# Gated-delta stages: another order of the steps of the four compute engines

## The chip, the cores and the metric

The kernel runs on one core of one Trainium2 chip. The metric is device time in microseconds (us). Before the change it is 2894.6 us, the median of three runs (2892.34 to 2895.38).

## What is computed

Two small transformers, one after the other, on 256 tokens of width 1024, in float32. The first has four layers, each a SwiGLU feed-forward, a mixer and a second feed-forward; the mixers are gated delta, stick-breaking attention, sparse attention and again gated delta. The second has two layers of another mixer and a squared-ReLU feed-forward. The change touches the two gated-delta mixers alone. Of one:

```python
proj = h @ w_in                                             # 1024 -> q, k, v, z (1024 each), b, a (8 each)
qkv = silu(causal_depthwise_conv(proj[..., :3072], conv_w)) # 4 taps
q, k = l2norm(q) * 128 ** -0.5, l2norm(k)
beta = sigmoid(b); g = -exp(a_log) * softplus(a + dt_bias)
# chunk by chunk: decay = exp(segment sums of g) below the diagonal
lower = where(strict, beta * (k @ k.T) * decay, 0)
sol = triangular_solve(lower + eye, [v * beta, k * beta * exp(g_cum)])
# u = u_in - w @ state; o = q_dec @ state + (q @ k.T * decay) @ u; state = state * g_tot + k_dec.T @ u
o = rmsnorm(o, norm_g) * silu(z)
return o @ w_out
```

## The kernel before

**Stages.** The program is a list of 16 stages (line 3142 on); the gated-delta stages are the second and the eleventh. Each compute engine has, for each stage, a written-out list of steps; `run` (line 237) walks it and advances one generator ("lane") per word. A lane's `yield` ends a step. Engines meet only at semaphores, and each engine works its own queue strictly in the order of its list. What stands behind an instruction that waits does not start.

**The W lane.** Weights come in pieces of 1 MB through a ring of five buffers. For each piece SyncE loads `raw`, ScalarE makes `hi` (line 638), VectorE the rest `lo` (line 656; GpSimd at line 676 for five late pieces of a gated-delta stage), and TensorE multiplies in three products. On TensorE a W step is half a piece: in the q, k and v columns 24 matmuls of 256 columns (lines 503 to 505, piece by piece in `tensor_cols`), in the z and output columns 12 matmuls of 512 (lines 430 to 432). On ScalarE and VectorE every other W step prepares the piece that is three pieces ahead. A stage has 21 pieces, so 42 W steps: W1 to W10 make k and the two gate columns, W11 to W18 q (q0, q2, q4, q6, two steps each), W19 to W26 v, W27 to W34 z, W35 to W42 the output.

**PSUM banks.** TensorE takes one of eight banks for every product it starts (`take`, line 212): the next one in a ring, skipping only banks that are still being filled. A bank that is full but not yet read is not skipped. TensorE then waits until its reader is done. So which earlier product a step waits for follows from the order of TensorE's list, and it changes when the list does.

**Steps of the gated-delta lanes.** `E.1` to `E.12` (VectorE line 1596, ScalarE line 1408) read one projected pair out of its bank: VectorE multiplies by the row norm (`cin`, line 1603), which frees the bank, ScalarE does the first tap, VectorE three taps for two columns (line 1609). E.1 to E.4 are k, E.5 to E.8 are q0, q2, q4, q6, E.9 to E.12 are v. `nk` and `nq` normalise k and q: the squares on ScalarE, a column sum on TensorE (line 1328), a root on ScalarE, the product on VectorE (line 1647). `c0` to `c3` are the four chains of the triangular solve, one for four heads of one half of the tokens; their steps are: .1 decay (VectorE 1671 and 1674, ScalarE's exponentials), .2 the product k k (VectorE 1684, then ScalarE's four copies into `goz`, called Z copies here), .3 to .6 the rest of the inverse. `inv.1` on VectorE (line 1718) transposes `goz` once the Z copies of all four chains are made, and GpSimd's `inv` (line 1786) then solves the small diagonal blocks. `inv.2` closes that. `kT` turns k; `rows` turns v; `qk` is q k; `a0` and `a1` apply the result; `gates` are the scalars per token and head.

Of the kernel before, what the change touches and what calls it, by code (L numbers as in the profile page):

```python
# [1231 lines left out]


GDN_PE = """
x1 W W rbc rbc W W W W W gates W W W gates gates gates gates W W c0 W c2 nk nk nk c3 W nk c0 nk W W c1 c2 kT c1 c3 W W
W W W W W kT W W nq nq nq W nq W W nq W W qk qk rows W W rows rows rows qk W W c2 c0 c1 c0 c2 c0 c1 c0 c2 c1 a0 c3 c2
a0 c3 a0 c3 c1 a0 a1 a0 c3 a1 a1 qk a0 a0 a1 W a1 W W a1 a1 W W W W next W gates gates nk nq
"""
GDN_ACT = """
x1 W W W rbc rbc E E ba W W gates gates E W W gates W W E W W nk E W W gates gates gates W W nk nk E nk nk c0 c2 W W  # L1240
c3 c2 c0 c1 c3 c1 E W W W W E W W kT E nq E nq W W E nq kT nq E nq sv W W Z W W rows rows c0 c2 c1 c3 Z c2 c0 rows
rows c1 gate W W c3 a0 a0 a0 a0 a0 a1 a1 a1 a0 a0 W W a1 a1 W W W W a1 a1 W W W W next W gates nk nq
"""
GDN_DVE = """
x1 clear rbc W W W E E gates W W gates E gates W W gates E W W gates gates W W E c2 c0 nk nk nk nk E nk nk c0 c3 W W
c2 c1 c3 c1 W W inv W W E W W E E W W E nq nq nq W W E nq E W W nq nq qk inv qk c0 qk c2 c1 c0 c2 c0 c1 c3 c0 gates c2
a0 c1 a0 c2 c3 a0 c3 c1 a0 a1 a0 a1 c3 a0 qk a1 a0 a1 a1 a1 a1 W W W W W W W W W W W W out out next W W out W W rbc W
"""
GDN_POOL = """
clear c0 inv W W W W W W W W W W W W W W W W W W W W W W W W W W W c2 c1 c3 W W W W W W W W W W W W W W W  # L1250
"""


# [1929 lines left out]
```

## Time and profile before

| | |
|---|---|
| median of three runs | 2894.6 us |
| span of the profiled execution, first to last instruction | 2891.6 us |
| TensorE busy | 2851.9 us (99%) |
| VectorE busy | 1795.2 us (62%) |
| ScalarE busy | 1578.0 us (55%) |
| GpSimd busy | 452.6 us (16%) |
| mean granted TensorE clock | 0.997 |

The profile is of one execution. Its device time is not listed apart from its span, which is 3.0 us below the median of the runs. In the rows PE is TensorE, DVE VectorE, ACT ScalarE, POOL GpSimd. A row gives start, length, engine, source line, operation, output and input, and in square brackets how long the engine had been idle and who released it. The first gated-delta stage covers about 193 to 371 us of the span, the second 1665 to 1843 us, 1472.6 us later.

### The profile page before, as it was taken

The page shows a single profiled execution, that of the slowest core. Times are in us where ns is not written, and L with a number is a line of the kernel's source. Part 1 is how long each engine was busy: PE and PEld are TensorE (multiplying, and loading weights), DVE is VectorE, ACT ScalarE, POOL GpSimd, SP SyncE. Part 2 cuts the span into 40 slices and gives each one's busy share as a digit, 9 for nine tenths or more (in the row PEclk, how much of TensorE's full clock was granted, in tenths as well). Part 3 has the DMA queues.
Part 4 walks back from the last instruction along what each step waited for, and adds up shares of the span by engine and source line. Part 5 has one row for each costly group of instructions (what it writes and reads, how often), then busy time and mean ns, then how long its engine had stood idle before and what let it go on. Part 6 is the DMA issues. An engine that isn't in the chain of part 4 may idle for free.

```text
span 2891.6 us, 35970 instructions
## 1 busy us (share of the span) xinstructions
PE 2851.9 (99%) x14255; PEld 2419.0 (84%) x14255; DVE 1795.2 (62%) x2190; ACT 1578.0 (55%) x1982; POOL 452.6 (16%) x700
## 2 busy tenths in 40 slices
PE   9999999999999999999999999999999999999998
PEld 7888888888988888878888898888888888888887
DVE  5558666565666556466556487566675665775664
ACT  5448854544554454565444388643566463566462
POOL 1203512021002112041202107121000020000020
PEclk9999999999999999999999999999999999999999
DMA  8764267576548677537767653476645686645684
GB/s 277 234 191 129 88 218 239 195 247 214 173 155 245 214 227 238 181 117 225 227 207 241 200 159 117 133 247 212 200 147 174 214 278 220 194 146 176 217 278 158
DMA packets 397047, 574.90 MB, mean 199 GB/s; under 512 B 20016, under 2 KB 248624, under 8 KB 396880
## 3 DMA queue, kind: packets, MB, share of 16 engines
q1 hardware_dynamic: 372624, 508.62, 54.7%
q0 software_dynamic: 23680, 62.95, 7.0%
q8 instruction: 112, 1.84, 0.3%
q10 hardware_dynamic: 576, 1.05, 0.1%
q14 instruction: 55, 0.45, 0.1%
HBM read 540.03 MB, written 32.51 MB: 198 GB/s over the span
## 4 chain that ended last, share of the span: by engine, by line
PE 87%; DVE 6%; ACT 4%; issue 1%; DMA 1%; SPq 0%; POOL 0%; DVEq 0%; ACTq 0%
PE ps L430 26%; PE ps L432 26%; PE ps L431 26%; PE ps L616 2%; DVE lo L656 2%; DVE qkv L1609 2%; PE ps L503 1%; PE ps L505 1%; PE ps L504 1%; ACT goz L1400 1%; PE ps L587 1%; ACT hi L638 1%; PE ps L603 1%; ACT sl L1400 1%; ACT qkv L1400 0%
## 5 line engine op out<-in xcount | busy, mean ns | idle before, releaser
L656 DVE TENSOR_TENSOR lo<-raw,hi 128x2048 fp32r<-128x2048 f32 (+3 forms) x473 | 1052.6, 2238 | 451.0 <-ACT hi L638 451.0
L638 ACT ACTIVATE hi<-raw 128x2048 fp32r<-128x2048 f32 (+2 forms) x487 | 907.4, 1871 | 766.6 <-DMA raw<-in_ffn_w_gu 283.7
L430 PE MATMUL ps<-hi,xh 128*128 128x512 f32 (+1 forms) x2208 | 865.8, 392 | 3.3 <-DVE xl L812 2.4
L432 PE MATMUL ps<-hi,xl 128*128 128x512 f32 (+1 forms) x2208 | 858.4, 389 | 0.0
L431 PE MATMUL ps<-lo,xh 128*128 128x512 f32 (+1 forms) x2208 | 857.8, 388 | 0.0
L430 PEld LDWEIGHTS ps<-hi,xh 128*128 128x128 f32 x2208 | 415.0, 188 | 88.2 <-DVE lo L656 4.1
L432 PEld LDWEIGHTS ps<-hi,xl 128*128 128x128 f32 x2208 | 414.7, 188 | 85.8
L431 PEld LDWEIGHTS ps<-lo,xh 128*128 128x128 f32 x2208 | 415.1, 188 | 84.0 <-issue 1.0
L430 PE MATMUL ps<-hi,hhh 128*128 128x512 f32 x704 | 274.6, 390 | 0.0
L432 PE MATMUL ps<-hi,hhl 128*128 128x512 f32 x704 | 274.0, 389 | 0.0
L431 PE MATMUL ps<-lo,hhh 128*128 128x512 f32 x704 | 273.9, 389 | 0.0
L1009 POOL DMA_DIRECT2D hhr<-turned x352 | 191.3, 550 | 377.6 <-DMA turned<-hhf 368.7
L503 PE MATMUL ps<-xh,hi 128*128 128x256 f32 x672 | 195.9, 292 | 8.2 <-DVE cin L1603 8.2
L504 PE MATMUL ps<-xl,hi 128*128 128x256 f32 x672 | 191.8, 285 | 0.0
L505 PE MATMUL ps<-xh,lo 128*128 128x256 f32 x672 | 191.6, 285 | 0.0
L1005 POOL DMA_DIRECT2D turned<-hhf x88 | 49.7, 565 | 792.7 <-DVE hhf L993 792.3
L432 PEld LDWEIGHTS ps<-hi,hhl 128*128 128x128 f32 x704 | 132.1, 188 | 27.5
L431 PEld LDWEIGHTS ps<-lo,hhh 128*128 128x128 f32 x704 | 132.2, 188 | 27.2
L430 PEld LDWEIGHTS ps<-hi,hhh 128*128 128x128 f32 x704 | 132.2, 188 | 27.2
L1113 ACT ACTIVATE sg<-ps,st 128x256 f32<-128x256 f32 x176 | 78.8, 470 | 119.4 <-PE ps L432 119.2
L1028 DVE TENSOR_TENSOR hhl<-hhr,hhh 128x512 fp32r<-128x512 f32 x88 | 60.4, 687 | 128.0 <-ACT hhh L1017 99.2
L503 PEld LDWEIGHTS ps<-xh,hi 128*128 128x128 f32 x672 | 130.6, 194 | 10.5 <-DVE cin L1603 8.6
(440 smaller groups left out, 3403.3 us busy)
## 6 DMA issues: line engine op xcount, KB each, us to landing
raw<-in_ffn_w_gu SPq DMA_DIRECT2D x348, 512.0 KB, 4.8
raw<-in_ffn_w_down SPq DMA_DIRECT2D x80, 1024.0 KB, 5.0
raw<-in_w_ff SPq DMA_DIRECT2D x64, 1024.0 KB, 5.4
raw<-in_w_in SPq DMA_DIRECT2D x60, 1024.0 KB, 5.1
raw<-in_gdn_w_in SPq DMA_DIRECT2D x32, 1024.0 KB, 5.5
turned<-hhf POOLq DMA_DIRECT2D x88, 256.0 KB, 4.5
hhr<-turned POOLq DMA_DIRECT2D x352, 64.0 KB, 4.0
raw<-in_sb_w_in SPq DMA_DIRECT2D x12, 1024.0 KB, 5.1
```

The lines of the kernel that those rows point to most:

```text
L430: e.matmul(o, a1, r1, start=kk == 0, stop=False)
L431: e.matmul(o, a1, r2, start=False, stop=False)
L432: i = e.matmul(o, a2, r1, start=False, stop=kk == kts - 1)
L503: e.matmul(o, a1, x1, start=kk == 0 and q == 0, stop=False, skip_group_check=True)
L504: e.matmul(o, a1, x2, start=False, stop=False, skip_group_check=True)
L505: i3 = e.matmul(o, a2, x1, start=False, stop=kk == 7, skip_group_check=True)
L616: i = k.e.transpose(o, lhs(h), k.m.C(C_ID)) if turn else k.e.matmul(o, lhs(h), rhs(h), start=True, stop=True)
L638: k.e.activation(k.m.hi[q % RING][:, 0:n], k.m.raw[q % RING][:, 0:n], ACT.Copy).then_inc(*k.up("act_piece_hi", ("hi", q)))
L656: k.e.tensor_tensor(m.lo[i][:, 0:n], m.raw[i][:, 0:n], m.hi[i][:, 0:n].bitcast(F32), ALU.subtract).then_inc(*k.up("dve_piece_lo", ("split" ...
L1009: k.e.dma_start(f.raw[32 * b:32 * b + 32, c + 1, :].rearrange("i (a r) -> i a r", a=4), rows).then_inc(*k.up(f"dma_fetch{c % 3}", *([("fet ...
L1028: k.e.tensor_tensor(f.turned(f.low, c), f.back(c), f.turned(f.high, c).bitcast(F32), ALU.subtract).then_inc(*k.up("dve_turned_lo", ("hT", ...
L1113: k.e.activation(r["sg"][i][:, :], b.ps[:, 0:256], ACT.Silu, scale=m.st[:, 16 + t:17 + t]).then_inc(*k.up("act_ffn_silu", ("silu", g, c, t)))
```

## The change

All four lists of the gated-delta stages are replaced. Each engine has the same steps as before, in the same number, and within a lane in the same order; only the way in which the lanes are interleaved differs.

```diff
@@ -1232,22 +1232,23 @@
 
 
 GDN_PE = """
-x1 W W rbc rbc W W W W W gates W W W gates gates gates gates W W c0 W c2 nk nk nk c3 W nk c0 nk W W c1 c2 kT c1 c3 W W
-W W W W W kT W W nq nq nq W nq W W nq W W qk qk rows W W rows rows rows qk W W c2 c0 c1 c0 c2 c0 c1 c0 c2 c1 a0 c3 c2
-a0 c3 a0 c3 c1 a0 a1 a0 c3 a1 a1 qk a0 a0 a1 W a1 W W a1 a1 W W W W next W gates gates nk nq
+x1 W W rbc rbc W W W W W gates W W W W W gates gates gates gates c0 W nk nk W c2 nk c3 nk nk W c2 c0 c1 W c3 kT c1
+W kT W W W W W W nq nq W nq W nq W qk W nq W W W W qk W rows qk rows rows rows W W c0 c2 c1 c0 c2 c0 c3 c1 c0 c2 a0
+c3 c1 a0 c2 a0 c3 c1 a0 a1 a0 c3 a1 a1 qk a0 a0 a1 W a1 W W a1 a1 W W W W next W gates gates nk nq
 """
 GDN_ACT = """
-x1 W W W rbc rbc E E ba W W gates gates E W W gates W W E W W nk E W W gates gates gates W W nk nk E nk nk c0 c2 W W
-c3 c2 c0 c1 c3 c1 E W W W W E W W kT E nq E nq W W E nq kT nq E nq sv W W Z W W rows rows c0 c2 c1 c3 Z c2 c0 rows
-rows c1 gate W W c3 a0 a0 a0 a0 a0 a1 a1 a1 a0 a0 W W a1 a1 W W W W a1 a1 W W W W next W gates nk nq
+x1 W W W rbc rbc E E ba W W gates W W E gates gates W W E W W nk E W W nk W W gates gates gates nk E nk W W c0 c2
+nk c0 c3 c2 c1 c3 c1 E W W E W W kT E nq W W E kT W W nq nq W W E nq W W E nq sv Z rows rows c0 c2 c3 c1 Z c0 c2
+rows rows c1 W W c3 W W gate a0 a0 a0 a0 a0 a1 a1 a1 a0 a0 a1 a1 a1 a1 W W W W W W next W W W gates nk nq
 """
 GDN_DVE = """
-x1 clear rbc W W W E E gates W W gates E gates W W gates E W W gates gates W W E c2 c0 nk nk nk nk E nk nk c0 c3 W W
-c2 c1 c3 c1 W W inv W W E W W E E W W E nq nq nq W W E nq E W W nq nq qk inv qk c0 qk c2 c1 c0 c2 c0 c1 c3 c0 gates c2
-a0 c1 a0 c2 c3 a0 c3 c1 a0 a1 a0 a1 c3 a0 qk a1 a0 a1 a1 a1 a1 W W W W W W W W W W W W out out next W W out W W rbc W
+x1 rbc clear W W W E E gates W W gates E gates W W E gates W W gates gates W W E c0 c2 nk nk nk E nk c3 nk c0 c2 nk
+W W c1 c3 c1 W W W W inv E E E W W E W W nq nq nq nq E W W nq W W gates E nq qk qk inv c0 c2 c1 qk c0 c2 c0 c3 c1
+c0 c2 a0 c1 a0 c2 c3 a0 c1 a0 c3 a1 a0 c3 a1 a0 a1 a0 qk a1 a1 a1 a1 out W W W W W W W W W W W W out next out W W W
+W W rbc
 """
 GDN_POOL = """
-clear c0 inv W W W W W W W W W W W W W W W W W W W W W W W W W W W c2 c1 c3 W W W W W W W W W W W W W W W
+clear c0 c2 inv W W W W W W W W W W W W W W W W W W W W W W W W W W W c1 c3 W W W W W W W W W W W W W W W
 """
 
 
```

Positions by the number of W steps ahead of a step, before and after, of those that the text below speaks of. TensorE: kT.2 23 and 17; gates.5 10 and 12; nq.2 25 and 23; qk.1 30 and 26; rows.1 30 and 32. ScalarE: nk.5, c0.1 and c2.1 15 and 17; E.12 25 and 29; gate 29 and 33. VectorE: c2.2 (13 to 11), inv.1 (15 to 17), E.8 and E.9 (19 to 17), E.12 (23 to 25), out.1 (37 to 25). GpSimd: c2.1, 27 to 0 and ahead of `inv`.

## Rows read from the trace of the kernel before

**Rows 1.** Busy time, share and instructions of each engine, whole span.

```profile
PE 2851.9 (99%) x14255; PEld 2419.0 (84%) x14255; DVE 1795.2 (62%) x2190; ACT 1578.0 (55%) x1982; POOL 452.6 (16%) x700
```

**Rows 2.** Waits of TensorE, whole span: us in total, times, longest.

```profile
PE ps L503 <- DVE cin L1603: 8.2, 2, 4.1
...
PE ps L1319 <- DVE ga L1633: 1.6, 2, 0.8
...
PE ps L1328 <- ACT sy L1400: 1.0, 3, 0.6
```

**Rows 3.** Timeline of TensorE, 248 to 270 us: start, length.

```profile
250.07 0.36 PE L503 MATMUL ps<-xh,hi 128*128 128x256 f32 x1
...
261.55 0.28 PE L505 MATMUL ps<-xh,lo 128*128 128x256 f32 x1
265.95 0.58 PE L503 MATMUL ps<-xh,hi 128*128 128x256 f32 x1 [4.12 <-DVE cin L1603]
...
269.26 0.28 PE L503 MATMUL ps<-xh,hi 128*128 128x256 f32 x1
```

**Rows 4.** Timeline of VectorE, 246 to 266 us.

```profile
246.30 2.28 DVE L656 TENSOR_TENSOR lo<-raw,hi 128x2048 fp32r<-128x2048 f32 x1
...
255.82 1.13 DVE L1684 SCALAR_TENSOR_TENSOR sl<-ps,ga,sl 128x128 f32<-128x128 f32 x4 [3.04 <-ACT sl L1400]
...
261.88 1.25 DVE L1718 STREAM_TRANSPOSE gow<-goz 128x1024 f32<-128x1024 f32 x1 [2.73 <-ACT goz L1400]
263.05 2.25 DVE L656 TENSOR_TENSOR lo<-raw,hi 128x2048 fp32r<-128x2048 f32 x1
265.22 0.68 DVE L1603 TENSOR_TENSOR cin<-ps,rbc 128x512 f32<-128x512 f32 x1
```

**Rows 5.** Timeline of ScalarE, 239 to 262 us.

```profile
239.06 0.91 ACT L1400 ACTIVATE qkv<-cin,vec 128x256 f32<-128x256 f32 x2 [0.57 <-DVE cin L1603]
239.88 0.67 ACT L1400 ACTIVATE sy<-ps,const 128x512 f32<-128x512 f32 x1
...
242.35 0.62 ACT L1400 ACTIVATE sl<-sl 128x512 f32<-128x512 f32 x1
...
244.53 1.90 ACT L638 ACTIVATE hi<-raw 128x2048 fp32r<-128x2048 f32 x1
...
249.65 5.49 ACT L1400 ACTIVATE goz<-sl 32x256 f32<-32x256 f32 x8 [2.18 <-DVE sl L1684]
255.16 0.63 ACT L1400 ACTIVATE sl<-sl 128x512 f32<-128x512 f32 x1
...
256.31 5.53 ACT L1400 ACTIVATE goz<-sl 32x256 f32<-32x256 f32 x8
```

**Rows 6.** Stretches of the second stage: busy us by engine, PEclk, DMA, GB/s.

```profile
1732.00:1742.00 10.00, 5.89 (x37) 5.68 (x36) 6.94 (x10) 5.84 (x8) 5.34 (x11) 0.75 0.46 154
1742.00:1752.00 10.00, 10.00 (x79) 10.00 (x79) 8.84 (x13) 7.35 (x12) 8.75 (x17) 0.91 0.34 107
```

**Rows 7.** Timeline of TensorE, 310 to 319 us: last z piece, first chain step.

```profile
310.64 0.48 PE L430 MATMUL ps<-hi,xh 128*128 128x512 f32 x1
...
316.21 1.95 PE L616 MATMUL ps<-sl,sl 128*128 128x128 f32 x16
318.66 1.16 PE L616 MATMUL ps<-sl,sl 128*128 128x128 f32 x8 [0.51 <-ACT zs L1400]
```

**Rows 8.** Timeline of ScalarE, around 310 and 357 us.

```profile
310.63 7.27 ACT L1400 ACTIVATE sl<-gow 32x128 f32<-32x128 f32 x16 [0.33 <-DVE gow L1727]
...
357.39 1.55 ACT L897 ACTIVATE goh<-ps,vec 128x256 fp32r<-128x256 f32 x4
```

**Rows 9.** Timeline of VectorE at 306 us: the sum that closes the inverse.

```profile
306.15 4.45 DVE L1727 TENSOR_TENSOR gow<-gow 128x512 f32<-128x512 f32 x1
```

**Rows 10.** Timeline of GpSimd, 255 to 310 us.

```profile
255.22 1.29 POOL L1783 TENSOR_TENSOR sl<-sl,const 128x512 f32<-128x512 f32 x1 [10.32 <-ACT goz L1400]
...
305.44 4.60 POOL L676 TENSOR_TENSOR lo<-raw,hi 128x2048 fp32r<-128x2048 f32 x1 [1.63 <-ACT hi L638]
```

## The prediction, made before the changed kernel was run

> **What bounds the kernel now.** I read the busy shares first: TensorE is busy for 2851.9 us, 99% of the span [rows 1]. No order of steps can shorten its work; what can change is the time in which it waits, and the slower clock behind a long wait. So I read its waits next [rows 2]. The longest in a gated-delta stage, 8.2 us in two times, is of a projection matmul (line 503) for VectorE's `cin`, one in each of the two stages. The timeline shows it [rows 3]: the matmul before it starts at 261.55, the next at 265.95, where 0.12 us is the spacing of the others (96 matmuls, W17 to W20, lie between 250.07 and 261.55). Until 269.26 fifteen matmuls start 0.22 us apart: the lower clock level costs 3.31 - 15 x 0.12 = 1.5 us. In the second stage the clock is low for longer: granted 0.75 over one stretch of 10 us and 0.91 over the next [rows 6]. At the two levels of 2.4 and 1.2 GHz, 0.25 x 10 / 0.5 = 5.0 us and 0.09 x 10 / 0.5 = 1.8 us were low, some of it idle.
>
> What ended the wait, on VectorE's queue [rows 4]: W21 (v2) takes the bank that q4 (W15, W16) had filled, and q4 is read by E.7. E.7's `cin` stands behind a weight split (263.05), and that behind inv.1's transpose, which had waited 2.73 us for ScalarE's Z copies, over at 256.31 + 5.53 = 261.84 [rows 5].
>
> **The change, the decisive part: kT.2.** kT.2 moves on TensorE from behind W23 to behind W17. I counted banks through both lists. Before, it took the bank of c2's kk product, read long ago; now the ring gives it the bank after q6's (W17), and that one holds q4, which only E.7's `cin` reads. W21 now takes c0's kk bank, which is read at once, and W19 that of c2. So the same event, E.7's `cin`, releases TensorE in both orders. Before, W18, W19 and W20 were done by then. Now they are behind it.
>
> Call the release R. Before, R = 265.95. The work that is moved behind it is three W steps, 72 matmuls x 0.12 = 8.65 us (kT.2 itself is only exchanged against the place that it had). The change breaks even at this point if R comes 8.65 us earlier.
>
> When is R? E.7 follows inv.1, and inv.1 the sixteen Z copies of four chains. I follow ScalarE from E.6, whose `cin` comes at nearly the same time in both orders, to 239.06 [rows 5]. Queue in the new order until the first Z copies: E.6 0.82, root 1.24 (half of 242.35 - 239.88), weight `hi` 1.81, c0.1 and c2.1 2.18, root 1.24: 7.3, so 246.4. VectorE has c0's product at 246.2: after E.6's taps (241.8) come two normalisations of 0.6, c3's decay of 2.1 and the product, 1.13 [rows 4]; and the split of 246.30 [rows 4], which stood ahead of c2.2, is now behind both. So ScalarE's wait of 2.18 us [rows 5] is gone, and the first Z copies start at 246.4 instead of 249.65. From there ScalarE has 16 copies, 5.49 + 5.53 = 11.0, the exponentials of c3, 1.05, and of c1, 1.15 (256.31 - 255.16): to 259.6. VectorE's products of c3 and c1 are ready in time (c1's at about 254.9) and its two splits (2 x 2.2) end near 259.3. Then transpose 1.2, `cin` 0.7 with no split between, and the semaphores: R = 261.7. It gains 2.2 from the split and 2.1 from the Z copies, 4.25 in all, and I need 8.65. Net +4.4 us in each stage. The two ends for R: nothing gained by the Z copies, 263.8, net +6.5; Z copies with another 2 us less, 259.7, net +2.4. I take the middle since every term has a row.
>
> The wait itself becomes long, from 253 or so to 261.7, 8 to 9 us. The lower clock level behind it: the rows show 1.5 us lost behind a wait of 4.1 us, and more in the second stage behind the same wait [rows 3, 6], so its length is not what sizes the loss. I take the loss as before, 0 more; if it were in proportion to the wait, 1.5 to 2 more each stage.
>
> On that the Trainium skill has a rule (TensorE: Matmul & The Clock Gate, section What's actually happening): the clock falls to half after idling and returns once the engine has been busy for a while, so a longer wait costs no more slow matmuls behind it. By that the sum stays +4.4; by proportion it would be near +6. The unequal losses behind equal waits speak for the rule, and the sum does without it.
>
> **The parts costed at nothing.** Whatever is ahead of R on TensorE is worth nothing. That holds for gates.5 behind W12 (it removes a wait of 0.8 us each, [rows 2]) and for nk.5, now ahead of c0.2: its sum must wait about 2 us for ScalarE. Both end in the long wait. Without that cover they would be -0.8 and +2. GpSimd's c2.1 ahead of `inv`: GpSimd was idle 10.32 us before c0's [rows 10], so it fits. Behind `inv` it spares 1.8 us, but ScalarE's copies of the finished inverse into the chains (310.63, [rows 8]) waited for the closing sum, not for GpSimd, so 0; with that cover gone, up to -1.8.
>
> The closing sum took 4.45 us [rows 9] beside GpSimd's split of 4.60 [rows 10]. Now that split waits for E.12, whose taps end near 306, and the sum comes at 312 to 313.5. The Trainium skill (SBUF — State Buffer, section SBUF: two separate sides) says that a VectorE operation with two SBUF inputs and a GpSimd operation that reads SBUF exclude each other for a whole instruction; the trace agrees (4.45 us for a sum that ends with GpSimd's split at 310.04). By that rule the sum comes at 313.5, by free flow at 312. ScalarE gets to its copies at 314.7 either way, so neither changes the sum.
>
> **Behind R.** Being late, TensorE no longer waits for ScalarE's squares (0.6 and 0.2 us in the first stage, 1.0 in three times over both [rows 2]): -0.5 to -0.8. I take -0.7. Then each W step's split must be ready. VectorE now does E.7, E.8, E.9 in a row, and E.9 needs W20: 261.7 + kT.2 0.6 + 8.65 + slow clock 1.5 to 2 = 272.8. The splits that TensorE needs at W25, W27, W29 and W31 end by my walk at 280.7, 289.3, 299.1 and 302.4, (E.9's taps and a split; E.10 and a split; two normalisations, E.11 and a split; one more of each), and TensorE is there at 286, 293.6, 299.8 and 305.3. W29's has 0.7 us to spare. Cost 0; if VectorE is 1 to 3 us later, up to +2.5.
>
> The last z steps end at 320.0 instead of 316.21 [rows 7]. The chain's first product then finds its operand: ScalarE starts the 7.27 us of copies at 314.7, held by rows.2 (TensorE does rows.1 behind W32, at 312), ends at 322.0, does Z.2 and the copy for c0.4, 323.9. TensorE arrives at c0.4 at 323.0 and waits 0.9, where before it waited 0.5 [rows 7] and again 0.4 near this place: the same. From here on the chain steps interleave with one or more others between a product and its user as before: 0, bounds -0.5 to +0.5.
>
> At the end: VectorE's out.1 now stands ahead of one split for the next stage (2.3 us, needed only some 5 us later): 0. ScalarE's `hi` for the last output piece moves behind a1.7: `goh` 1.55 [rows 8], `hi` 1.9, GpSimd's split 4.6 [rows 10] are 8.05 us, while TensorE does three W steps of half of (316.21 - 310.64), 8.35. It just fits: +0.1, up to +1.
>
> **Sum.** Each stage +4.4 - 0.7 + 0.1 = +3.8. Both stages: +7.6. The profiled span goes from 2891.6 to 2899.2 us. The span is 3.0 us below the median of the runs; I let that difference stand: 2902.2 us.
>
> **Rivals.**
> 1. *A pile-up behind R.* VectorE and GpSimd, pushed behind W20 and E.12, miss W29, W31 or W33. Speaks for it: 0.7 us to spare, and taps that are slower beside GpSimd's `inv`. Against: ScalarE and VectorE have gaps to catch up in. +2.5 to +6 a stage more: 2907 to 2914.
> 2. *The delay is absorbed, no change within 0.2%.* R comes at 260 (-1.7 each), or the chain steps behind W34, which wait for nothing TensorE does late, come without their 0.9. 2 x (3.8 - 1.7 to 2.6) = +2.4 to +4.2: 2897 to 2899.
> 3. *Faster: R comes before its price.* Place: `cin` of E.7. It decides at R = 265.95 - (8.65 - 0.7 + 0.1) = 257.9. The Z copies would have to end at 255.8, and their own 13.2 us to start at 242.6, before the exponentials that feed them are made; R = 256.6 would give -1.3 a stage, 2892.0 in all. Only if kT.2's bank weren't q4's would it happen: then TensorE meets no gate, 4.1 + 1.5 to 2.2 + 0.7 a stage, about -13 in all: 2881. Against it: the ring gives bank after bank, and I find no step that would shift it.
>
> Chances: the forecast 0.60, rival 1 0.12, rival 2 0.21, rival 3 0.07. A measurement here tells about 0.2% (5.8 us) from no change. The forecast's own range is 2898 to 2907; its part below 2900.4 goes to "same", so slower 0.68, same 0.26, faster 0.06. The range that should hold the time 8 times in 10 is 2896.5 to 2909: it leaves out rival 3, most of rival 1, and takes in both ends for R (2 x (2.4 - 0.6) = +3.6 and 2 x (6.5 - 0.6) = +11.8).
>
> **What would show it.** In the changed kernel's trace TensorE should wait 8 to 9 us, twice, in front of a transpose of `qkv` (line 616), released by `cin` of line 1603, and no longer in front of line 503. E.7's `cin` should start at 261.0 and end at 261.7. The Z copies should start near 246.4 and end near 259.6. The last z matmul should start near 320. The waits of line 1319 should be gone, one of line 1328 of about 2 us should be there ahead of W15. The prediction is wrong if the wait is elsewhere, if R is before 259 or after 264, or if TensorE waits again for splits (line 656 or 676) between 273 and 320.

## The result, and the profile after

The changed kernel takes 2914.2 us (median of five runs, 2912.5 to 2914.4), against 2894.6 before (now also five runs): ratio 1.0070, 95% interval 1.0059 to 1.0081. It is slower, as forecast, but by 19.6 us where I forecast 7.6, and outside the range of 2896.5 to 2909. Behind the changed list the lines of the code have numbers one higher than before.

The busy times answer to [rows 1]; TensorE's work has not grown. Its waits (us in total, times, longest) answer to [rows 2].

```profile
PE 2854.1 (98%) x14255; PEld 2422.4 (83%) x14255; DVE 1793.2 (62%) x2190; ACT 1576.8 (54%) x1982; POOL 442.8 (15%) x700
```

```profile
PE ps L616 <- DVE cin L1604: 15.1, 2, 7.6
PE ps L616 <- ACT zs L1401: 11.8, 2, 6.0
...
PE ps L1329 <- ACT sy L1401: 3.7, 3, 1.2
```

The first line is the wait that I forecast. The second isn't: 6.0 us in each stage, for ScalarE's Z.2, where before it was 0.5 us [rows 7]. TensorE's timeline in the first stage has both, answering to [rows 3, 7]:

```profile
260.54 1.11 PE L616 MATMUL ps<-const,qkv 128*128 128x128 f32 x4 [7.56 <-DVE cin L1604]
...
265.72 0.33 PE L505 MATMUL ps<-xh,lo 128*128 128x256 f32 x1
265.89 0.28 PE L503 MATMUL ps<-xh,hi 128*128 128x256 f32 x1
...
282.02 1.10 PE L1329 MATMUL ps<-sy,const 128*128 128x512 f32 x2 [1.22 <-ACT sy L1401]
...
320.59 0.39 PE L432 MATMUL ps<-hi,xl 128*128 128x512 f32 x1
326.79 4.44 PE L616 MATMUL ps<-sl,sl 128*128 128x128 f32 x21 [5.81 <-ACT zs L1401]
```

Kernel before, the same two places of the chains (end of z on TensorE; VectorE's first reading of a chain product), and VectorE's first steps of inv.2:

```profile
315.99 0.39 PE L432 MATMUL ps<-hi,xl 128*128 128x512 f32 x1
```

```profile
303.96 0.87 DVE L1723 TENSOR_SCALAR goz<-gov,const 128x512 f32<-128x512 f32 x2
...
321.51 0.69 DVE L1660 SCALAR_TENSOR_TENSOR sl<-ps,sl 128x512 f32<-128x512 f32 x1 [0.98 <-PE ps L616]
```

So the last z matmul starts 320.59 - 315.99 = 4.6 us late, and the chain's product is read 332.57 - 321.51 = 11.1 us late (row below). The first matmul of the stage behind starts at 386.21 instead of 375.13, again 11.1: it is all there by the first chain product, 4.6 ahead of it and 6.5 in front of it. In the second stage the same two places stand at +2.2 and +8.8, counted from the delay that the first left: less was lost anew ahead of the chains, and 6.6 at them. Sum 19.9; the spans differ by 19.8 (2911.4 and 2891.6).

Why less ahead of the chains in the second stage? Mostly the clock. Counted at 0.12 us a matmul, the slow ones behind the wait lost 1.5 us before (15 of them) and 2.1 after (21) in the first stage, but 2.4 before (24, from 1738.56 to 1743.81) and 1.1 after (10, from 1744.99 to 1747.25) in the second. That is 1.9 of the 2.4 us between +4.6 and +2.2.

What ended the second wait is on VectorE, ScalarE and GpSimd, changed kernel, answering to [rows 9], [rows 8] and [rows 10]:

```profile
258.67 1.25 DVE L1719 STREAM_TRANSPOSE gow<-goz 128x1024 f32<-128x1024 f32 x1 [0.25 <-ACT goz L1401]
259.83 0.65 DVE L1604 TENSOR_TENSOR cin<-ps,rbc 128x512 f32<-128x512 f32 x1
...
310.16 0.69 DVE L1711 TENSOR_TENSOR qkD<-ps,qkD 128x512 f32<-128x512 f32 x1 [3.99 <-PE ps L616]
310.77 3.15 DVE L1724 TENSOR_SCALAR goz<-gov,const 128x512 f32<-128x512 f32 x2
313.95 1.25 DVE L1726 STREAM_TRANSPOSE gow<-goz 128x1024 f32<-128x1024 f32 x1
315.24 3.68 DVE L1728 TENSOR_TENSOR gow<-gow 128x512 f32<-128x512 f32 x1
...
332.57 0.69 DVE L1661 SCALAR_TENSOR_TENSOR sl<-ps,sl 128x512 f32<-128x512 f32 x1 [3.97 <-PE ps L616]
```

```profile
318.95 7.07 ACT L1401 ACTIVATE sl<-gow 32x128 f32<-32x128 f32 x16 [3.14 <-DVE gow L1728]
326.05 1.26 ACT L1401 ACTIVATE zs<-ps,st 128x512 f32<-128x512 f32 x2
```

```profile
305.05 4.99 POOL L676 TENSOR_TENSOR lo<-raw,hi 128x2048 fp32r<-128x2048 f32 x1 [11.59 <-DVE qkv L1610]
309.98 0.52 POOL L1782 MEMSET sl<- 128x512 f32 x1
...
312.19 1.45 POOL L1784 TENSOR_TENSOR sl<-sl,const 128x512 f32<-128x512 f32 x1
313.59 4.77 POOL L676 TENSOR_TENSOR lo<-raw,hi 128x2048 fp32r<-128x2048 f32 x1
```

inv.2 is the multiplications, the transpose and the closing sum. The multiplications take 3.15 us instead of 0.87, beside GpSimd's clears and chain steps. The sum takes 3.68 us and ends at 318.9, just behind GpSimd's *second* split (313.59 + 4.77 = 318.36), which had started 1.65 us ahead of it. ScalarE's copies, held by the sum, run from 318.95, and Z.2 comes behind them.

What put the two side by side is in part argued. inv.2 starts 6.8 us later than before (310.77 against 303.96), behind a `qk` product that TensorE makes only behind W31. With c2.1 gone from GpSimd's queue the second split starts some 1.7 us earlier (a clear and a chain step, 309.98 to 311.70); with c2.1 in its place it would start near 315.3 by that estimate, and the sum started at 315.24. Which of the two would have come first isn't shown: no run has GpSimd's old list beside the other new ones.

Why TensorE needs Z.2 for its first chain products (c0.3 and c2.3) is again the ring of banks. Counted through both lists: before, the products of c2 and c0 take banks of `qk` and `rows`, read early, and only c1's takes a bank of z's second half, which Z.2 reads. In the new order c0's and c2's products themselves get the two banks of that half.

The clock around both waits, by the windows (busy us by engine, PEclk, DMA, GB/s):

```profile
250.00:260.00 10.00, 2.98 (x25) 2.78 (x24) 9.37 (x19) 8.36 (x15) 2.24 (x3) 0.78 0.26 90
260.00:270.00 10.00, 9.46 (x60) 9.46 (x61) 6.18 (x13) 3.62 (x5) 8.22 (x23) 0.71 0.24 60
321.00:326.00 5.00, 0.00 (x0) 0.00 (x0) 0.00 (x0) 4.73 (x12) 0.00 (x0) 0.78 0.69 208
326.00:331.00 5.00, 4.21 (x21) 4.21 (x22) 2.48 (x4) 2.28 (x5) 0.00 (x0) 0.53 0.00 2
```

TensorE idles in the third stretch, and in the fourth it works at 1.2 GHz almost throughout.

### The profile page after: what moved, and what is told of

The parts are those of the page before. It is cut to its first block, busy times and chain, and to the rows that moved or that the text cites. A ratio compares the mean times of both kernels' runs of the same rounds, so it can differ in the third digit from the quotient of the medians.

```text
span 2911.4 us, 35976 instructions
## 1 busy us (share of the span) xinstructions
PE 2854.1 (98%) x14255; PEld 2422.4 (83%) x14255; DVE 1793.2 (62%) x2190; ACT 1576.8 (54%) x1982; POOL 442.8 (15%) x700
## 4 chain that ended last, share of the span: by engine, by line
PE 90%; ACT 4%; DVE 4%; issue 1%; DMA 1%; SPq 0%; POOL 0%; DVEq 0%; ACTq 0%
PE ps L430 26%; PE ps L432 26%; PE ps L431 26%; PE ps L616 3%; PE ps L503 2%; PE ps L504 2%; PE ps L505 2%; DVE lo L656 1%; ACT goz L1401 1%; DVE qkv L1610 1%; PE ps L587 1%; ACT hi L638 1%; ACT sl L1401 1%; PE ps L603 1%; ACT qkv L1401 0%
```

## The experiments

The theory: two gates in each stage, each a bank in the ring. One is kT.2 for E.7's `cin`. The other is the first chain products for Z.2, and Z.2 is late since inv.2 runs beside GpSimd. The rival: the delay of kT.2 alone costs everything, and the wait at the chains is only its echo. The runs come from three rounds, in which the kernel before took 2893.0, 2893.5 and 2893.2 us; between rounds the ratios are compared, not the times. The fences of the edits show only the places that change, and with the edits line numbers shift by up to six.

To move a bank without moving any work, TensorE gets a word `skip`, which passes over one bank of the ring:

```diff
+    def skip():
+        for _ in range(script.count("skip")):
+            k.c.next += 1
+            yield
```

**kt_skip: one bank passed over ahead of kT.2.**

```diff
 GDN_PE = """
 ...
-W kT W W W W W W nq nq W nq W nq W qk W nq
+W skip kT W W W W W W nq nq W nq W nq W qk W nq
```

> The changed kernel (2914.2 us) with one bank of the ring passed over ahead of kT.2 on TensorE, so that kT.2 no longer takes the bank that holds q4; all lists as changed. Theory 1, the bank gate at kT.2 carries a good part of the slowdown: the wait of 7.6 us in front of kT.2 is gone, a shorter one (4 to 5 us) comes in front of nq.2's sum, the last z matmul starts 4 to 6 us earlier, and the time falls by 7 to 11 us to 2903 to 2907. Theory 2, the late end of the inverse and of ScalarE's copies sets the time and TensorE only waits for it in one place or another: the wait in front of the chain's first products grows by what is won, and the time stays at 2911 to 2915.

Measured 2910.0 (ratio to before 1.0053, 1.0038 to 1.0067). TensorE, first stage:

```profile
275.61 2.04 PE L1328 MATMUL ps<-sy,const 128*128 128x512 f32 x2 [4.57 <-ACT sy L1405]
...
316.38 0.39 PE L432 MATMUL ps<-hi,xl 128*128 128x512 f32 x1
323.31 2.93 PE L616 MATMUL ps<-sl,sl 128*128 128x128 f32 x12 [6.54 <-ACT zs L1405]
```

The 7.6 us are gone, and z ends 4.2 us earlier. But 4.57 us come back at nq.2's sum, and at the chains TensorE waits 6.54 us instead of 5.81, so that the first chain product starts 3.5 us earlier and the next stage 2.65 (383.56 against 386.21). The second wait doesn't go with the first: it is no echo. The gain over both stages is 0.0017, some 5 us where I expected 7 to 11, and the intervals of this run and of the changed kernel overlap.

**et_skip: banks passed over ahead of the chain products alone.**

```diff
-rows rows W W c0 c2 c1 c0 c2 c0 c3
+rows rows W W skip skip c0 c2 c1 skip skip skip c0 c2 c0 c3
```

> The changed kernel with two banks passed over ahead of c0.3 and three ahead of c0.4 on TensorE, so that the first three chain products (c0, c2, c1 ET) take banks whose readers are long done, and not those of z's second half, which Z.2 reads. Theory 1, the banks of z hold these products back: the wait of 5.8 us falls to about 0.5 in front of the first and shorter ones behind it, the slow clock behind it is gone, X1 of c0 starts about 3 us earlier; 2906 to 2909. Theory 2, the operands (all sixteen copies of the inverse end at 326.05) hold the chain back anyway: under 1.5 us a stage, 2911 to 2914.

Measured 2914.9 (1.0074, 1.0057 to 1.0091): no gain. TensorE's waits and its timeline in the first stage say why:

```profile
PE ps L616 <- DVE qkD L1716: 9.9, 2, 4.9
```

```profile
319.84 1.13 PE L616 MATMUL ps<-sl,sl 128*128 128x128 f32 x8
321.61 1.13 PE L616 MATMUL ps<-sl,sl 128*128 128x128 f32 x8 [0.65 <-issue]
...
327.67 6.87 PE L616 MATMUL ps<-sl,sl 128*128 128x128 f32 x40 [4.93 <-DVE qkD L1716]
```

I had miscounted by one: c1's product now took the bank of the third `qk`, which VectorE reads behind inv.2. The edit took away one gate and made another, so it tells nothing of the gate's price. It does tell what held the first two products: with other banks they start at 319.84 and 321.61, right behind z, while ScalarE is still making the sixteen copies (317.95 to 325.04). In the changed kernel it was the bank that they waited for, not the operand.

**inv_first: inv.2 ahead of the second `qk` on VectorE.**

```diff
-nq qk qk inv c0 c2 c1 qk
+nq qk inv qk c0 c2 c1 qk
```

> The changed kernel with inv.2 ahead of the second qk step on VectorE, as before the change; nothing else. Theory 2, the inverse ends late because inv.2 stands behind a product that TensorE makes only behind W31, and then runs beside GpSimd's splits (3.15 and 3.68 us where 0.87 and 0.7 would do): the closing sum ends near 311 instead of 318.9, ScalarE starts its copies near 315.3, set by rows.2, Z.2 comes 3.6 us earlier, and TensorE's wait falls from 5.8 to 2 us; 2914.2 - 2 x (3.6 to 4.5) = 2905 to 2907. Theory 1 alone (banks, not the inverse) would leave 2912 to 2914, since Z.2 would be held by something else.

Measured 2913.3 (1.0067, 1.0052 to 1.0082), no gain clear of the scatter. In the first stage inv.2 starts 5.5 us earlier and ends 0.9 us earlier. VectorE, then GpSimd:

```profile
305.22 6.57 DVE L1723 TENSOR_SCALAR goz<-gov,const 128x512 f32<-128x512 f32 x2
...
313.11 4.91 DVE L1727 TENSOR_TENSOR gow<-gow 128x512 f32<-128x512 f32 x1
```

```profile
304.18 4.99 POOL L676 TENSOR_TENSOR lo<-raw,hi 128x2048 fp32r<-128x2048 f32 x1 [10.32 <-DVE qkv L1609]
...
312.88 4.58 POOL L676 TENSOR_TENSOR lo<-raw,hi 128x2048 fp32r<-128x2048 f32 x1
```

The same three instructions take 12.8 us. In the second stage of the same execution the closing sum begins 0.35 us ahead of the split instead of 0.23 behind it:

```profile
1795.66 0.94 DVE L1727 TENSOR_TENSOR gow<-gow 128x512 f32<-128x512 f32 x1
```

```profile
1796.01 5.06 POOL L676 TENSOR_TENSOR lo<-raw,hi 128x2048 fp32r<-128x2048 f32 x1
```

There it takes 0.94 us and not 4.91, and the wait at the chains is 2.63 us, where in the first stage it is 5.78. Moving inv.2 up the queue gains nothing by itself, as GpSimd's instructions come beside it there too; what counts is which of the two starts first. (The profiled execution, at 2910.4 us, is the fastest of the four; the others took 2912.7 to 2914.1.)

**all3: these three edits together.**

> The changed kernel with all three edits: bank passed over ahead of kT.2, banks passed over ahead of c0.3 and c0.4, inv.2 ahead of the second qk on VectorE. If the two bank waits and the late inv.2 are the whole of the slowdown, their gains add: 2888 to 2897, about the time before the change. If something else in the lists costs time (ScalarE's order of E.12 and rows), it stays at 2900 or more.

Measured 2906.8 (1.0045, 1.003 to 1.006). The gates of et_skip (4.93 us at c1's product) and of kt_skip (4.6 at nq.2) are both still there.

**u_wait: inv_first, and GpSimd's late splits wait until the closing sum is done.**

```diff
-pool_pieces(k, plan, g, ("conv", g, 22))
+pool_pieces(k, plan, g, ("U", g))
```

> The changed kernel with inv.2 ahead of the second qk on VectorE, and GpSimd's late weight splits held until the closing sum of the inverse is made (they wait for that sum instead of for E.12's taps). Theory 3: VectorE's three steps of inv.2 take 14 us because they run beside GpSimd's split, chain steps and second split, which the late E.12 has moved onto them; with GpSimd idle they take 2.8 us (0.87, 1.25, 0.7), the closing sum ends near 308, ScalarE's copies start at about 315 behind rows.2 and end at 322, TensorE's first chain product starts near 322.8 instead of 326.8 and without the slow clock behind it: 5 to 6 us a stage, 2902 to 2905. If something else makes inv.2 late, the steps stay long and the time stays at 2910 to 2914.

Measured 2906.8 (1.0047, 1.0032 to 1.0062). VectorE and GpSimd:

```profile
306.04 0.88 DVE L1723 TENSOR_SCALAR goz<-gov,const 128x512 f32<-128x512 f32 x2
...
308.23 0.69 DVE L1727 TENSOR_TENSOR gow<-gow 128x512 f32<-128x512 f32 x1
```

```profile
309.00 4.58 POOL L676 TENSOR_TENSOR lo<-raw,hi 128x2048 fp32r<-128x2048 f32 x1 [15.60 <-DVE gow L1727]
```

With GpSimd idle the three take 0.88, 1.25 and 0.69. ScalarE's copies now start at 315.6, held by `rows` on TensorE, and the wait at the chains is 2.69 us (2.67 in the second stage) instead of 5.81 (5.97), 6.4 less in both. The price of the two engines side by side is 0.0020 of the time against inv_first, which differs in this alone, and 0.0023 against the changed kernel: 6 to 7 us.

**kt_inv_u: u_wait and kt_skip together.**

> The same with one bank passed over ahead of kT.2. The bank gate won 3.5 us in front of the chains in kt_skip and gave it back to the late inverse. If theory 3 is right the two now add: the last z matmul ends near 316.8, ScalarE's copies start near 311.5, the first chain product near 319.5 (released by Z.2), 2896 to 2900. If the gate's gain is lost in another way it is 2902 or more.

Measured 2895.8 (1.0010, 1.0000 to 1.0020; ten runs): 11 us less than u_wait, where kt_skip by itself gave some 5. With inv.2 undisturbed, what is won at the first gate reaches the chains (the first product starts at 318.33 instead of 323.61) and stays.

**fix_all: kt_inv_u, and banks passed over ahead of the chain products, now counted rightly.**

```diff
-rows rows W W c0 c2 c1 c0 c2
+rows rows W W skip skip c0 c2 skip c1 skip skip c0 c2
```

> The same, and banks passed over ahead of c0.3, c1.3 and c0.4 so that the chains' first products take banks that are read (not z's, nor that of the third qk, which VectorE reads late). If the three causes (bank gate at kT.2, the late and slow inv.2, the banks of z in front of the chains) are the whole of the slowdown, the time is that of before, 2891 to 2896; if not, 2898 or more.

Measured 2892.5 (0.9999, 0.9989 to 1.0008; ten runs). The engines keep the changed kernel's order of work but for inv.2's place and GpSimd's held splits, and the time is that of before. TensorE:

```profile
316.54 0.39 PE L432 MATMUL ps<-hi,xl 128*128 128x512 f32 x1
316.77 1.95 PE L616 MATMUL ps<-sl,sl 128*128 128x128 f32 x16
318.96 1.13 PE L616 MATMUL ps<-sl,sl 128*128 128x128 f32 x8 [0.24 <-issue]
```

**only_pe and only_act: one list of the four in the kernel before.**

```diff
 # only_pe
-GDN_PE = (the list of before)
+GDN_PE = (the list of the change)
 # only_act: the same with GDN_ACT
```

> The kernel before with TensorE's new list alone; ScalarE, VectorE and GpSimd as before. By the bank count kT.2 waits for E.7's cin, which VectorE's old list gives at 265.9: a wait of about 12 us in front of kT.2, W18 to W20 behind it, so +8.6 us a stage less 1 for later waits. Theory of the bank gate: 2906 to 2912. If the order of VectorE and ScalarE made the slowdown and TensorE's not: 2894 to 2898.

Measured 2943.4 (1.0174, 1.0159 to 1.0190), far above what I expected:

```profile
PE ps L616 <- DVE cin L1603: 27.0, 2, 13.5
PE ps L1328 <- ACT sy L1400: 17.4, 4, 5.9
```

kT.2 waits 13.5 us, where I expected 12, and TensorE waits another 17.4 us in all for ScalarE's squares, for which I had nothing. The old lists bring E.7 at their own pace. So the new lists of the other engines give back nearly half of this wait, and TensorE's list makes it.

> The kernel before with ScalarE's new list alone. On it E.12's first tap stands behind two more weight copies (W28, W29) and nq.5 behind it; VectorE, in the old order, waits for that tap and everything behind it, inv.2 too, comes late, and GpSimd's first split (which waits for E.12) moves onto inv.2. Theory: 1 to 5 us a stage, 2896 to 2904, with inv.2's steps on VectorE longer than 3 us. If ScalarE's list is harmless by itself: 2892 to 2895.

Measured 2913.2 (1.0069, 1.0055 to 1.0082). VectorE and GpSimd:

```profile
310.34 5.62 DVE L1723 TENSOR_SCALAR goz<-gov,const 128x512 f32<-128x512 f32 x2
```

```profile
305.56 7.77 POOL L676 TENSOR_TENSOR lo<-raw,hi 128x2048 fp32r<-128x2048 f32 x1 [0.79 <-DVE qkv L1609]
```

I expected 2904 at most. The mechanism that I expected, slow multiplications, is there, and three other waits of 2.0 to 3.9 us in each stage besides, for VectorE's decay (line 1674) and twice for ScalarE's squares. So neither TensorE's nor ScalarE's new list works with the others of before. VectorE's and GpSimd's lists by themselves weren't tried.

**old_skip: the kernel before, one bank passed over ahead of W21.** This asks what the old gate [rows 2, 3] was worth.

```diff
-W W W W W kT W W nq nq nq
+W W skip W W W kT W W nq nq nq
```

> The kernel before with one bank of the ring passed over ahead of W21, so that W21 doesn't take the bank that holds q4. The wait of 4.1 us in front of it goes in both stages. If that wait carried time: 2 x (4.1 + 1.5 to 2.2) less, 2881. If ScalarE's squares for nq.2 carry it, the wait reappears in front of line 1328 as some 5 us with the slow clock behind it: 2891 to 2893.

Measured 2893.3 (1.0002, 0.9993 to 1.0011). W21's wait is gone, and 5.6 us come back at kT.2, where I thought of nq.2. The time stays, as expected if ScalarE's queue carries it:

```profile
PE ps L616 <- ACT kd L1405: 11.1, 2, 5.6
```

**nq_late: fix_all with W24 ahead of nq.2. rows_early: nq_late, and rows.1 and rows.2 ahead of W32, so that the copies start earlier.**

```diff
 # nq_late
-nq nq W nq W nq W qk
+nq W nq nq W nq W qk
 # rows_early
-qk W rows qk rows rows rows W W skip skip c0 c2 skip c1 skip skip c0
+qk rows rows W qk rows rows W W skip skip c0 c2 c1 skip skip skip c0
```

> fix_all (2892.5 us) with W24 ahead of nq.2 on TensorE. fix_all waits 4.6 us in front of nq.2's sum for ScalarE's squares, with the slow clock behind it (granted 0.67 over 10 us). One W step (2.9 us) in that place leaves 1.7 us of wait and no slow clock: 3 to 4.5 us a stage, 2884 to 2887, if TensorE carries the time there. If ScalarE's and VectorE's queues carry it, what is won comes back as a longer wait in front of the chains, and it stays at 2890 to 2893.

Measured 2890.7 (0.9989, 0.9981 to 0.9998; eleven runs). Windows of nq_late, then of fix_all:

```profile
273.00:278.00 5.00, 3.31 (x17) 2.18 (x17) 3.15 (x3) 4.97 (x7) 4.53 (x7) 1.00 0.58 168
278.00:283.00 5.00, 2.32 (x20) 2.12 (x18) 4.89 (x7) 4.97 (x10) 4.45 (x8) 0.95 0.12 46
283.00:288.00 5.00, 4.79 (x16) 3.76 (x17) 3.50 (x5) 4.61 (x8) 4.45 (x8) 0.50 0.00 0
```

```profile
273.00:278.00 5.00, 2.49 (x6) 1.49 (x7) 3.15 (x3) 4.97 (x7) 4.53 (x7) 0.68 0.00 2
278.00:283.00 5.00, 5.00 (x25) 4.52 (x25) 4.88 (x7) 4.97 (x10) 4.45 (x8) 0.64 0.02 3
```

The wait of 4.6 us became one of 1.69 (up to 275.50) and one of 2.89 us (up to 283.21), as many us together. Behind the first the matmuls come 0.12 us apart, at full clock; behind the second they come 0.21 apart until 289.3, a slow stretch as long as fix_all's. Of the 6 to 9 us over both stages that I expected, 2 to 3 are there, and the intervals overlap.

> nq_late with rows.1 and rows.2 ahead of W32 on TensorE (banks passed over so that the chains' first products still take banks that are read). In fix_all ScalarE stood idle 2.7 us for rows.1's product while the inverse was ready 6 us before its copies began. The copies should begin 2 to 3 us earlier. If they end the chain: 1.5 to 3 us a stage less than nq_late, 2878 to 2884; if TensorE's own steps up to W34 end later than the copies, nothing, the same as nq_late.

Measured 2889.8 (0.9988, 0.9979 to 0.9997; eleven runs). The first chain product starts at 314.21 without a wait, 2.8 us ahead of nq_late (317.02), and the next stage 4.2 us ahead (371.68 against 375.84). Only 0.9 us of the median is left of that. The profiled executions show where it goes: the 4.2 us are kept for 800 us, 1.1 are lost by 1311 and 1.8 more between 2007 and 2097, in stages that the edit doesn't touch, and the second gated-delta stage adds only 0.2. Why these stages take it back stays open. It is the fastest version that ran, 0.12% under the kernel before: real by its interval, and about half of what I called measurable.

## Why the prediction was wrong

**Right, by its steps.** kT.2 and its bank: TensorE waits for E.7's `cin` at line 616, twice, 7.56 us, and no longer at line 503. R is 260.5 (forecast 261.7); the Z copies end at 258.6 (259.6), `cin` at 260.5 (261.7). The waits of line 1319 are gone, and one of line 1328 is there ahead of W15 (1.25 us, forecast 2). The splits were ready in time: between R and the end of z no wait for a split. The clock behind the wait: the slow matmuls lost 2.1 us in the first stage and 1.1 in the second, where behind a wait of half the length they lost 1.5 and 2.4. That is as the rule of the Trainium skill has it (TensorE: Matmul & The Clock Gate, section What's actually happening), and not in proportion.

The last z matmul starts at 320.6 (320.0). Up to there the forecast of +3.7 a stage was +4.6 in the first and +2.2 in the second, 6.8 together where it had 7.4. That this is so near is partly luck. In the first stage the work behind R less the earlier release came to +3.2 and not +4.4, as R was 1.2 us early; against that the clock cost 0.9 more than before (0.6 on the W steps, 0.3 on kT.2), where I had 0; and the -0.7 for ScalarE's squares wasn't there: TensorE waits 1.22 us for them at 282.02, where before it was 0.8 in all, +0.4.

**The step that failed** is that the late inverse and the first products of the chains cost nothing: the passages from "neither changes the sum" (the parts costed at nothing) to "the same" (behind R). It has two faults.

First, the bound on inv.2. I weighed the closing sum beside *one* split of GpSimd, from 312 to 313.5, and left out the multiplications before it. Measured, inv.2 took 8.2 us and ended at 318.9. The rule that I quoted there (the Trainium skill, SBUF — State Buffer, section SBUF: two separate sides) held for the sum, which again ended with GpSimd's split. But each VectorE instruction of inv.2 should have been set beside every GpSimd instruction from 305 to 320, the second split too. u_wait shows this fault at 6 to 7 us over both stages.

Second, the banks of the chain products. I counted the ring for kT.2, which decided the sign, and for the chains I took the old owners: "finds its operand", "waits 0.9". The operand was there (et_skip); the bank wasn't. With the right owners, but my time for the copies (322.0 and Z.2, 323.3), the wait would have been near 3 us (323.3 less 320.4), and u_wait and kt_inv_u show 2.7. From kt_inv_u to fix_all this fault is worth 3 us over both stages.

Together they make 5.4 us of wait more than before in each stage, and by subtraction 1.1 us of slow clock: 13.1 us at the chains of both stages where I had nothing. Less the 0.6 that came out lower ahead of the chains, and the 0.2 that I had put at the end and that isn't to be seen, that is the 12.2 us, within 0.1, by which the spans' difference passed my sum.

Rival 1 had the size (2907 to 2914, the result lies at its end) at a chance of 0.12, but not the place: it named the splits at W29 to W33, and these held. Rival 3's price for a kT.2 without q4's bank, 2881, was far off: kt_skip is that kernel, and it took 2910.0.

The gates also aren't a sum of prices. Taken away in turn they gave 0.0023, 0.0037 and 0.0011 of the time (6.7, 10.7 and 3.2 us); the 10.7 are 5 or so when taken first. With both gates undone (fix_all) the ratio is back from 1.0070 to 0.9999. One doubt about that return is that fix_all holds GpSimd's splits, which the kernel before doesn't, and the kernel before wasn't run with that edit. At the closing sum it could win little by it: ScalarE was idle only 0.33 us for the sum there [rows 8]. What isn't shown: which move of the lists brought inv.2 and GpSimd's instructions together. ScalarE's new list does it alone for the multiplications (5.62 us in only_act, with GpSimd's old list); what c2.1's move adds stays open. And it is counted in the traces, but not tested by a run, that the second stage lost less for the sake of the clock.

## What to carry to other kernels

When TensorE's list changes, recount the ring of PSUM banks through the whole stage, for every product the old owner of its bank, that owner's last reader, and what stands ahead of the reader on its queue; a wait for a bank looks like a wait for data. When the lists of VectorE or GpSimd change, set GpSimd's instructions beside each VectorE instruction of the critical path, and ask which starts first. And a wait taken away by itself may give little (kt_skip) or nothing (old_skip) since another wait takes its place: undo them together before you call one worthless.

## What the runs showed of the hardware

- Two VectorE multiplications by a constant, 128x512 each, take 0.88 us with GpSimd idle and 3.15, 5.62 and 6.57 us beside GpSimd's clears, chain steps and splits (the changed kernel, only_act, inv_first); they have one tensor as input, so this isn't only a matter of sums of two tensors. The sum took 0.69 alone and 3.68, 4.45 and 4.91 beside a split that had started before it. The transpose between them took 1.25 in all of these runs.
- Who starts first pays least: in inv_first a sum that began 0.35 us ahead of the split took 0.94 us and the split 5.06; one that began 0.23 behind it took 4.91 and the split 4.58.
- It costs GpSimd too: a split of 4.58 us took 4.99 beside VectorE instructions, and in only_act 7.77.
- Waits of 4.1, 4.6, 5.8 and 7.6 us were all followed by a stretch at 1.2 GHz, and the one of 7.6 lost about as much as the one of 4.1. A wait of 2.89 us was too, for as long; behind one of 1.69 us, 7.7 us ahead of it, the matmuls came at full clock.
